# Two stacked transformer blocks on one core: the Fourier mixing spread over the first attention's steps, its bias tables shared, four modulation pieces moved

## The reference, cut to what matters

```python
mod = (silu(c) @ w_mod[l] + b_mod[l])                 # shift, scale, gate vectors
u   = modulate(rms_norm(h, norm1_g[l]), sh1, sc1)
f, q, k, v = split(u @ w_in)                          # 512 columns each
kc, vc     = split(uc @ w_in[:, k and v])             # 256 context tokens
q, k, kc   = rms_norm of each head (8 heads of 64)
# Fourier mixing: 4 groups of 128 channels
mixed  = fft2(f of a group, over tokens and channels).real
o_four = mixed @ w_four[g]
# attention: each query sees an 8 x 16 window of the 8 x 64 grid and the context
s      = q k^T * scale + bias(rpb);  outside the window -inf
p      = softmax([s_window, q kc^T * scale])
o_na   = p_win v + p_ctx vc
y      = concat(o_four, o_na) @ w_out
h      = h + g1 * y
```

## Time and profile before

| | us |
|---|---|
| runs | 1969.67, 1970.55, 1962.75 (median 1969.67) |
| profiled execution, its own time | 1971.28 |
| its span, first to last instruction | 1969.5 |
| PE busy | 1932.1 (98%) |
| PE weight loads busy | 1587.5 (81%) |
| DVE, ACT, POOL busy | 967.1, 685.3, 944.7 |
| mean granted clock of PE | 0.993 |

### The profile page before, as it was taken

How to read it: one execution, slowest core, us unless ns; L and a number is a source line. 1 busy time by engine, 2 the same in 40 slices (tenths; PEclk the granted TensorE clock), 3 DMA queues, 4 the chain that set the end, 5 groups by cost and what they waited for, 6 DMA issues and landing times. The chain is left out here.

```text
span 1969.5 us, 25202 instructions
## 1 busy us (share of the span) xinstructions
PE 1932.1 (98%) x9932; PEld 1587.5 (81%) x9932; DVE 967.1 (49%) x1515; ACT 685.3 (35%) x907; POOL 944.7 (48%) x699
## 2 busy tenths in 40 slices
PE   7998999999999999999999999999999999999998
PEld 6875787888888888888888667888888888888886
DVE  4666849783755762232333562467654462222132
ACT  4232733121223432221233554456554342122222
POOL 3334365665656454545474213434444464545454
PEclk9999999999999999999999999999999999999999
DMA  8553133744542322222313012221212222232211
GB/s 328 189 171 136 44 150 130 276 171 149 192 153 82 147 86 99 93 107 85 107 64 135 24 42 102 86 85 66 86 65 86 107 86 107 86 107 86 107 64 43
DMA packets 42786, 223.11 MB, mean 113 GB/s; under 512 B 12737, under 2 KB 13249, under 8 KB 17345
## 3 DMA queue, kind: packets, MB, share of 16 engines
q1 hardware_dynamic: 42688, 221.77, 30.8%
HBM read 217.55 MB, written 2.10 MB: 112 GB/s over the span
## 5 line engine op out<-in xcount | busy, mean ns | idle before, releaser
L1011 POOL TENSOR_TENSOR wl<-raw,wh 128x512 fp32r<-128x512 f32 x611 | 862.3, 1442 | 955.1 <-ACT wh L557 842.1
L1116 PE MATMUL bank<-uh,wh 128*128 128x512 f32 x1416 | 564.6, 399 | 2.6 <-POOL wl L1011 2.2
L1118 PE MATMUL bank<-uh,wl 128*128 128x512 f32 x1416 | 552.7, 390 | 0.0
L1117 PE MATMUL bank<-ul,wh 128*128 128x512 f32 x1416 | 552.5, 390 | 0.0
L557 ACT ACTIVATE wh<-raw 128x2048 fp32r<-128x2048 f32 (+1 forms) x148 | 279.4, 1888 | 571.4 <-PE bank L1118 562.3
L1116 PE MATMUL bank<-ah,wh 128*128 128x512 f32 x848 | 331.2, 391 | 1.1 <-DVE al L1973 1.1
L1117 PE MATMUL bank<-al,wh 128*128 128x512 f32 x848 | 330.4, 390 | 0.0
L1118 PE MATMUL bank<-ah,wl 128*128 128x512 f32 x848 | 330.2, 389 | 0.0
L1116 PEld LDWEIGHTS bank<-uh,wh 128*128 128x128 f32 x1416 | 266.1, 188 | 69.0 <-issue 10.2
L1117 PEld LDWEIGHTS bank<-ul,wh 128*128 128x128 f32 x1416 | 266.3, 188 | 56.5 <-issue 3.6
L1118 PEld LDWEIGHTS bank<-uh,wl 128*128 128x128 f32 x1416 | 266.2, 188 | 56.2
(11 more groups left out here) (285 smaller groups left out, 2117.5 us busy)
## 6 DMA issues: line engine op xcount, KB each, us to landing
raw<-in_w SPq DMA_DIRECT2D x64, 1024.0 KB, 4.8
mraw<-in_w_modr SPq DMA_DIRECT2D x36, 1024.0 KB, 4.8
raw<-in_w_gu SPq DMA_DIRECT2D x22, 1024.0 KB, 4.8
raw<-in_w_hg SPq DMA_DIRECT2D x16, 1024.0 KB, 4.8
raw<-in_w_in SPq DMA_DIRECT2D x8, 1024.0 KB, 9.5
modf<-in_w_modf SPq DMA_DIRECT2D x8, 1024.0 KB, 20.5
raw<-in_w_out SPq DMA_DIRECT2D x8, 1024.0 KB, 5.0
raw<-in_w_dn SPq DMA_DIRECT2D x8, 1024.0 KB, 4.8
```

What stands on the lines that cost most here:

```text
L1011: pool.tensor_tensor(wl[:, slot, c + k:c + k + 2], raw[:, b % RAW, k:k + 2], f32(wh[:, slot, c + k:c + k + 2]), ALU.subtract).then_inc(spl ...
L1116: pe.matmul(out, ah_, bh, start=first, stop=False)
L1117: pe.matmul(out, ah_, bl, start=False, stop=False)
L1118: return pe.matmul(out, al_, bh, start=False, stop=last)
```

## The change

- The Fourier mixing is no stage of its own. `fourier_step(i)` stands behind each attention step: y of group 0, 1, 2, 3 in steps 1, 5, 9, 13, and its output in two parts in the two steps after. All of it uses bank 1; scores rotate over banks 4, 5, 0. High and low parts follow in step i + 3 of ACT and DVE.
- The channel tables are made in two parts, behind the first half of block 7 and in step 0.
- Window positions 1 and 2 have the same table, so two items share one (`table_of`, `table_last`): twelve pairs instead of sixteen. POOL makes a table once the normalisation before it is done as well.
- Pieces 6 to 9 lose their buffers and join pieces 0 to 5 (`MOD_EARLY` = 10).
- The tables `dftc`, `dfts`, `ff`, `ysb`, `cw` and `mask` move into slots of `raw`, and SP fetches them as slots come free; w_out blocks 9 to 11 are loaded after the last Fourier output.
- Front: the x sum is made on PE from each square, its factor is a row; vectors and bias are fetched after x, and w_in block 0 after the first `modf`; block 0 is split on ACT after the first rows; the root's table is loaded ahead.

```diff
-COLUMNS = ("x", "ctx", "pool")
+COLUMNS = ("ctx", "pool")
-MOD_EARLY, MOD_MID = 6, 10
+MOD_EARLY = 10
...
-        S_BANKS = [(4, 5), (0, 1)]
+        S_BANKS = (4, 5, 0)
+        def s_bank(i, e):
+            return bank[S_BANKS[(2 * i + e) % 3]]
+        def table_of(i):
+            return 3 * (i // 4) + (0, 1, 1, 2)[i % 4]
+        def table_last(t):
+            return 4 * (t // 3) + (0, 2, 3)[t % 3]
+        Y_STEP = {1: 0, 5: 1, 9: 2, 13: 3}
...
             sp.dma_start(con[:, 0:C_END], t["consts"]).then_inc(const_in, 16)
-            sp.dma_start(vec[:, 0:V_END], t["vecs"]).then_inc(const_in, 16)
-            sp.dma_start(bmod[:], t["b_mod"]).then_inc(const_in, 16)
             for i in range(2):
                 sp.dma_start(h[:, 4 * i:4 * i + 4, :], t["xT"][:, 4 * i:4 * i + 4, :]).then_inc(x_in[i], 16)
-            load(0, t["w_in"][0])
+            sp.dma_start(vec[:, 0:V_END], t["vecs"]).then_inc(vec_in, 16)
+            sp.dma_start(bmod[:], t["b_mod"]).then_inc(vec_in, 16)
             for i in range(8):
                 sp.dma_start(modf[:, i], t["w_modf"][i]).then_inc(modf_in[i], 16)
+                if i == 0:
+                    load(0, t["w_in"][0])
...
                 if b == 5:
                     sp.wait_ge(ctx_full, 4)
-                    sp.dma_start(dftc[:], t["dftc"]).then_inc(dft_in, 16)
-                    sp.dma_start(dfts[:], t["dfts"]).then_inc(dft_in, 16)
-                    mod_summed(sp, MOD_EARLY - 1)
                     sp.dma_start(cs[:], t["cs"]).then_inc(w4_in, 16)
                     sp.dma_start(w4[:], t["w4"]).then_inc(w4_in, 16)
+                    mod_summed(sp, MOD_EARLY - 1)
                     for c in range(QC):
                         sp.dma_start(tab[c::QC], t["rpb"][:, :, QC - 1 - c:QC - 1 - c + 48]).then_inc(tab_in, 16)
+            sp.wait_ge(split_hi, lows(6))
+            sp.wait_ge(split_lo, lows(6))
+            sp.dma_start(dftc[:], t["dftc"]).then_inc(dft_in, 16)
+            sp.dma_start(dfts[:], t["dfts"]).then_inc(dft_in, 16)
+            sp.wait_ge(split_hi, lows(7))
+            sp.wait_ge(split_lo, lows(7))
+            sp.dma_start(mask[:], t["mask"]).then_inc(tab_in, 16)
+            sp.wait_ge(smax, 2 * len(PAIRS))
+            load_mod(10)
+            load_mod(11)
+            sp.wait_ge(four_full, FG)
             load(9, t["w_out"][1])
-            for m in range(MOD_EARLY, MOD_MID):
-                load_mod(m)
...
+            load(10, t["w_out"][2])
+            load(11, t["w_out"][3])
+            load_mod(12)
+            load_mod(13)
...  ACT
-            act.wait_ge(const_in, 48)
+            act.wait_ge(const_in, 16)
+            act.activation(rc[:, 0, 0:1], eps_col, ACT.Sqrt)
             for k in range(KC):
                 h_wait(act, "x", k)
                 act.activation(sqx[:, k, :], h[:, k, :], ACT.Square).then_inc(sq_ready, 1)
-            split(0)
             root("x")
...
             rows_out(0)
+            split(0)
...
             for i in range(len(PAIRS) + 2):
+                if i - 3 in Y_STEP:
+                    four_high(Y_STEP[i - 3])
                 if i >= 2:
                     copy_pt(i - 2)
+                if i in Y_STEP:
+                    y_copy(Y_STEP[i])
                 if i < len(PAIRS):
                     exp(i)
...  POOL
+            def bias_table(t):
+                hp, w = t // 3, (0, 1, 3)[t % 3]
+                if t >= 2:
+                    last = table_last(t - 2)
+                    pool.wait_ge(smax, 2 * last + 2)
+                    if last:
+                        pool.wait_ge(p_norm, 2 * last)
+                for e in range(2):
...
+            bias_table(0)
+            bias_table(1)
+            fold(1)
+            split(8)
+            for t in range(2, 3 * len(PAIRS) // 4):
+                bias_table(t)
+                if t in (4, 7):
+                    fold(2 + (t - 4) // 3)
...  PE
             def sum_x():
-                pe.wait_ge(x_added, KC - 1)
-                for a in range(S // P):
-                    last = pe.matmul(bank[6][:, a:a + 1], sqx[:, KC - 1, P * a:P * a + P], ones_v[:, 0:1], ...)
+                for k in range(KC):
+                    pe.wait_ge(sq_ready, k + 1)
+                    last = rows(bank[6], sqx[:, k], k == 0, k == KC - 1)
+                    if k % 2 == 0:
+                        keep_clock(1)
                 last.then_inc(sum_full, 1)
...
-            keep_clock(22)
+            keep_clock(16)
             pe.wait_ge(csilp_ready, 1)
             sum_x()
             first_rows(0)
+            keep_clock(3)
+            first_columns(0)
             norm_spread("x")
-            first_columns(0)
+            keep_clock(6)
...
+            def fourier_step(i):
+                if i == 0:
+                    channel_tables(1)
+                if i in Y_STEP:
+                    fourier_y(Y_STEP[i])
+                for part in range(2):
+                    if i - 1 - part in Y_STEP:
+                        fourier_out(Y_STEP[i - 1 - part], part)
             def scores(i):
                 if i == 0:
-                    pe.wait_ge(four_lo, 4)
                     for n in range(len(HN)):
                         hn_wait_done(pe, n)
...
                 else:
-                    pe.wait_ge(smax, 2 * (i - 1))
+                    pe.wait_ge(smax, 2 * i - 1)
...
                 if 2 <= i < len(PAIRS) + 2:
                     turn(i - 2)
+                fourier_step(i)
...  DVE
-            for k in range(1, KC):
-                dve.tensor_tensor(sqx[:, k, :], sqx[:, k - 1, :], sqx[:, k, :], ALU.add).then_inc(x_added, 1)
...
-            mod_dot(MOD_EARLY)
-            mod_dot(MOD_EARLY + 1)
-            for g in range(FG):
...
+            channel_copy(0)
...
             for i in range(len(PAIRS) + 1):
                 if i < len(PAIRS):
                     row_max(i)
+                if i == 0:
+                    channel_copy(1)
                 if i >= 1:
                     normalise(i - 1)
+                if i - 3 in Y_STEP:
+                    four_low(Y_STEP[i - 3])
```

## The result

The kernel after takes **1975.64 us** (median of 11, 1972.06 to 1977.12) against 1969.50 for the kernel before (11 runs): ratio 1.0038, 95% interval 1.003 to 1.0047. I had said 1970.9, with 1958 to 1980 around it. The medians are 6.1 us apart.

The account below looks back on a forecast made before the run. PE was taken as the bound, busy 1932.13 of 1969.50 us. Terms -4.2 (front), -7.8 (Fourier filling), 0 (bias tables) and +13.2 (pieces) sum to +1.2, so 1969.7 becomes 1970.9; range 1958 to 1980, forecast alone 1965 to 1977.

Parts of the forecast that it names:

- the likeliest case: Whole kernel: the forecast itself, all terms summing to +1.2 us, median 1970.9 us; chance 60%.
- part 4: Block 4's start: DVE sums late pieces 6 to 9 ahead of hn_scale(0), PE waits 11.7 us; +13.2 in all, bounds +10 to +15.
- slow clock: Behind PE's wait at block 4: PE runs at the 1.2 GHz level for some 3.1 us, losing 1.5 us.
- part 1: Fourier mixing and attention: Fourier work fills twelve attention steps; net -7.8 us, bounds -9.5 to -5.5.
- The old place ... gives nothing back: Fourier stage: moving the reductions of pieces 6 to 9 away from beside PE's Fourier work saves nothing there.
- the tables in block 7: Block 7: half of the channel tables made there adds 1.0 us, 0.4 of it covering a wait; +0.6.
- the chain through bank 1: Attention, rival: y, output and their copies in one bank make each filled step wait 0.80; +9.6 us, 1980.5; chance 13%.
- Part 2: Attention: twelve bias-table pairs, each behind a normalisation, speed DVE's scalings; priced at 0 since PE sets the step.
- the rival in which DVE sets the step: Attention: a freed port shortens twelve steps by up to 0.58 us, 7 more in all, 1963.9; chance 10%.
- Part 3: Front: x sum by matmuls, reordered loads and splits; first scaled tile at 17.0; -4.2 us, bounds -2 to -5.5.
- block 1's split is then over: Front: the 1.44 us that first_columns(4) waited for ACT at 35.04 goes.
- The rival in which the pieces hold nobody: Block 4: pieces 6 to 9 are summed before hn_scale(0) is asked for, leaving -12.0, 1957.7; chance 17%.

Follow-up runs that it names:

- first experiment: Kernel after, with SP's loads of block 5 and pieces 6 to 9 ahead of the 32 vwin copies: 1957.40 us, ratio 0.9954.
- tenth: Kernel after, with DVE's sums of pieces 6 to 9 one behind each of hn_scale(0) to (3), SP's order unchanged: 1960.54 us, ratio 0.9963.
- fifth experiment: Kernel after, with SP's load of block 6 of w_in moved behind pieces 8 and 9: 1972.01 us, ratio 1.0013.
- sixth: Kernel after, with 54 idle 128x128 products on PE ahead of block 4's product: 1973.10 us, ratio 1.0024.
- second: Kernel before, with only all ten pieces put on the early list (MOD_EARLY = 10): 1980.27 us, ratio 1.0073.
- seventh: Kernel before, with all ten pieces on the early list and block 5 and the pieces ahead of the vwin copies on SP: 1964.93 us, ratio 0.9975.
- third experiment: Kernel after, without GpSimd's wait for the normalisation, each bias table made once its buffer is free: 1974.01 us, ratio 1.0033.
- fourth experiment: Kernel after, with 2 instead of 16 idle products on PE ahead of the row sums: 1972.69 us, ratio 1.0026.
- eighth: Kernel after, with ACT's split(1) moved behind the rows of the fourth vector: 1970.27 us, ratio 1.0018.
- ninth: Kernel after, with block 5 and pieces 6 to 9 ahead of SP's vwin copies and split(1) behind the fourth vector's rows: 1955.37 us, ratio 0.993.
- eleventh: Kernel after, with sums of pieces 6 to 9 behind hn_scale(0) to (3) and split(1) behind the fourth vector's rows: 1960.74 us, ratio 0.9961.

## Why the prediction was right or wrong

The time came out 4.7 us above the forecast, within 0.5% of the kernel before and inside the forecast's own range of 1965 to 1977; the likeliest case was the one that happened. That the range held is partly luck: part 4 (+17.55 with its slow clock, bounds +10 to +15) and part 1 (-10.07, bounds -9.5 to -5.5) both lie outside their own bounds, and their errors have opposite signs. The terms, with their own size:

- **What decides.** Right: part 4 decides. The sign of the whole hangs on it (first experiment), and its mechanism is the one given: DVE's sums wait for late pieces ahead of `hn_scale(0)` (first and tenth).
- **Part 4, size (+13.2).** The delay of block 4 was 15.23 and not 11.7. Counted from the same start the difference has three parts. Piece 8 landed 7.0 us after its issue, where I took 4.8 from transfers that had gone out on a free queue: +2.2; it went out at 107.10 behind block 6, which was still under way, and the fifth experiment brings it 2.5 us earlier. SP got only 1.6 of the front's 2.35 us (block 5 goes out at 97.14 instead of 98.74, behind 32 copies that took 21.60 instead of 20.78), so the pieces came later against PE's time than I put it: +0.8; the wait swallows what the front gains there. From landing to the end of the sums it took 8.02 and not 7.4: +0.6; a small add beside the split took 1.09 instead of 0.16. And the slow clock cost 2.3, not 1.5 (sixth).
- **"The old place ... gives nothing back".** This step failed. It gives back 4.1 us (second, seventh): with DVE's reductions gone from the stage, the POOL instructions that PE waited for took less time and the clock did not fall. The row was there, a wait of 2.25 us for `ff`, and DVE's 17.19 us in that stage; I read it as a price of the Fourier order and credited its end to part 1.
- **Part 1 (-7.8).** The mechanism is right, the size too small by 2.3 (73.8 predicted and 72.16 measured from w_in to w_out, and the 0.6 for the tables in block 7 did not show), and it was wrong in whose it was. The y of 1.8 was read from the weight load's row ahead of it; between the PE rows it is 1.40, in the kernel before as well (182.78 to 184.18). Of the -10.07 some 4.1 come with part 4 alone (second); the filling itself is worth 78.10 (the second experiment's 23.90 + 54.20) less 72.16 = 5.9. Two steps end with 0.80 of ACT's copy; the chain through bank 1 holds no filled step, so that rival falls. The tables in block 7 cost next to nothing: 51.25 (sixth) and 51.5 (first) against 51.23.
- **Part 2 (0).** Right. The third experiment shows that DVE's slower scalings do not reach PE, so the rival in which DVE sets the step falls; the sharing of tables was not tested by itself.
- **Part 3 (-4.2).** Mis-sized: -2.35. Two steps failed. The first scaled tile starts at 18.87, not 17.0, because PE's idle products stand ahead of the row sums (until 11.5) and the reciprocal of 128x128 takes 0.95 us; the fourth experiment shows that removing the first brings nothing, since the next transfer then holds PE. And "block 1's split is then over" was wrong: `split(1)` runs at 30.35 to 32.24, ahead of the very copy that PE waits for, and the 1.35 us stay (eighth). The -2.35 itself is one pair of executions. Three with the old front start the context products at 61.5, 62.2 and 64.0 us (second, before, seventh), six with the new one at 59.0 to 60.3 (after, first, third, fifth, sixth, tenth): the gain is there in every pair, but between 1.2 and 5.0 us.
- **The sum.** Every term but part 2 was off, by 1.9 to 4.4 us; errors of both signs left +5.1 where I had +1.2. The rival in which the pieces hold nobody was put at 1957.7; the kernel in which they do hold nobody is the first experiment, 1957.4. That is close by luck too: a front that gave less and an attention that gave more cancel.

## What to carry to other kernels

An instruction that waits for late data costs by what is queued behind it on its engine, so before a load is moved earlier, look at which ready instruction its consumer would stand in front of, and put the consumer behind that one or the load ahead of the small copies. When work leaves a stage, look also at which instructions of other engines it had slowed there. Take a transfer's time to landing from rows with the same load on the queue.

## What the runs showed of the hardware

**Behind the same short waits the clock fell in one run and not in another.** In the kernel after and in the fifth experiment PE has the same two waits for `wl`, of 0.9 and 1.23 us, at 74 and 76 us, with the same work ahead of them. The second wait, and windows of 76 to 80 us and of 1075 to 1100, the kernel after, then the fifth experiment:

```profile
76.08 0.39 PE L1147 MATMUL bank<-uch,wh 128*128 128x256 f32 x1 [1.23 <-POOL wl L1031]
...
76.00:80.00 4.00, 3.92 (x20) 3.92 (x21) 3.96 (x6) 0.00 (x0) 4.00 (x3) 0.58 0.87 293
1075.00:1100.00 25.00, 23.95 (x151) 20.23 (x149) 3.47 (x14) 8.12 (x12) 10.01 (x8) 0.93 0.20 80
```
```profile
76.47 0.39 PE L1149 MATMUL bank<-uch,wh 128*128 128x256 f32 x1 [1.23 <-POOL wl L1033]
...
76.00:80.00 4.00, 3.53 (x29) 3.54 (x30) 3.96 (x6) 0.00 (x0) 4.00 (x3) 1.00 0.90 282
1075.00:1100.00 25.00, 23.95 (x159) 20.16 (x158) 6.75 (x23) 9.33 (x18) 10.06 (x8) 1.00 0.18 60
```

The waits are the same; once the granted clock falls behind them and once it does not. It falls there in the kernel before too (0.79 and 0.78 over 76 to 80 and 80 to 84 us, 1.7 us in all) and not in the first experiment. Two more places lie behind w_out, where all kernels do the same work: 1075 to 1100 us, and 1150 to 1200 us (0.97). A clock of 0.93 over 25 us is 1.75 us, and 0.97 over 50 us is 1.5. From the first product of w_out to the end it takes 1722.6 to 1722.7 us where the clock falls in both (before, after, third), 1720.4 to 1721.4 where it falls in one (first, sixth, ninth) and 1719.2 to 1719.9 where it falls in neither (second, fourth, fifth, seventh, eighth, tenth, eleventh). With three such places a span moves by some 5 us.

The spread of the kernel before goes with it: of its 65 executions beside the experiments, the three with a mean granted clock of 0.999 have spans of 1960.7 to 1960.9 us and the two with 0.991 have 1971.6 and 1972.4, with the others in between. So a difference of a few us between two kernels of this study was taken from the stage that the edit touches, not from the medians. What tells a fall from none is open; no run was made for it.

**A late transfer and a busy queue.** The same 1 MB piece landed 4.8 us after its issue with no block ahead of it (fifth) and 7.0 with block 6 still under way (the kernel after). The Trainium skill ("DMA: Bandwidth & Descriptors", section "Queues, rings and completion order") says that on each DMA engine the descriptors of one ring are consumed in ring order. By that rule, the fifth experiment agrees; it does not tell such an order from two transfers that merely share the bandwidth.
